# Third mixture: token rows scattered to their expert slots tile by tile during the head

## What is computed

```python
def hierarchical_moe(t, w_group, b_group, w_inner, b_inner, w_gate, w_up, w_down):
    group_p = jax.nn.softmax((t @ w_group + b_group).astype(jnp.float32), axis=-1)
    g_w, g_idx = lax.top_k(group_p, 1)
    inner_all = jnp.einsum('nd,gde->nge', t, w_inner) + b_inner
    inner_logits = jnp.take_along_axis(inner_all, g_idx[:, :, None], axis=1)[:, 0]
    inner_p = jax.nn.softmax(inner_logits.astype(jnp.float32), axis=-1)
    e_w, e_idx = lax.top_k(inner_p, TOP_K_INNER)
    e_w = e_w / jnp.sum(e_w, axis=-1, keepdims=True)
    ...
    for g in range(N_GROUPS):
        hg = jax.nn.silu(jnp.einsum('nd,edf->nef', t, w_gate[g])) * jnp.einsum('nd,edf->nef', t, w_up[g])
        y = y + jnp.einsum('nef,efd->nd', hg * combine[:, g, :, None], w_down[g])
    return y
```

## Time and profile before

| | |
|---|---|
| median of the runs | 2281.05 us (2280.89 to 2281.74) |
| the profiled execution | 2284.3 us |
| its span, first to last instruction | 2282.5 us |
| mean granted clock of TensorE | 0.928 of full speed |
| TensorE matmuls busy | 2049.4 us, 90% |
| VectorE, ScalarE, GpSimd busy | 694.6, 340.2, 70.9 us |
| moved by DMA | 624.69 MB, 274 GB/s over the span |

### The profile page before, as it was taken

One profiled execution on the slowest core, in us unless ns is written; L12 is line 12 of the kernel. 1 busy time (PEld: TensorE's weight loads), 2 busy tenths in 40 slices (PEclk: granted clock), 3 DMA queues, 4 the chain that ended last, 5 costly groups with the idle time before them and its releaser, 6 DMA issues.

```text
span 2282.5 us, 25994 instructions
## 1 busy us (share of the span) xinstructions
PE 2049.4 (90%) x9962; PEld 1113.8 (49%) x9962; DVE 694.6 (30%) x1593; ACT 340.2 (15%) x758; POOL 70.9 (3%) x97
## 2 busy tenths in 40 slices
PE   7999889999999994999999999992899999879772
PEld 3444446555455542846455554451744664634441
DVE  0166646211111114345111111115416333412114
ACT  1133322000000000112000000000122330111110
POOL 0000000000000001000000000001100000100001
PEclk9999879999999997999999999996899559989996
DMA  9911102999999998413999999999222001589995
GB/s 336 360 42 38 56 3 93 399 420 421 421 421 422 421 421 313 148 58 135 412 419 421 421 421 421 421 421 320 69 89 74 1 19 40 224 350 421 420 421 215
DMA packets 144273, 624.69 MB, mean 274 GB/s; under 512 B 13265, under 2 KB 52273, under 8 KB 82769
## 3 DMA queue, kind: packets, MB, share of 16 engines
q1 hardware_dynamic: 119344, 567.24, 62.1%
q0 software_dynamic: 9504, 31.42, 4.1%
q10 hardware_dynamic: 15360, 25.18, 3.0%
HBM read 574.50 MB, written 49.28 MB: 273 GB/s over the span
## 4 chain that ended last, share of the span: by engine, by line
PE 74%; DMA 16%; DVE 6%; ACT 2%; issue 1%; POOL 0%; SPq 0%; POOLq 0%; ACTq 0%; DVEq 0%
PE bank L753 16%; PE bank L780 9%; PE bank L738 9%; DMA ring<-in_moe_w_up_dram 8%; PE bank L639 7%; PE bank L533 7%; DMA ring<-in_w_up_dram 5%; PE bank L504 5%; PE bank L545 4%; PE bank L762 3%; PE bank L892 2%; PE bank L908 1%; DVE h L1148 1%; PE bank L598 1%; PE bank L729 1%
## 5 line engine op out<-in xcount | busy, mean ns | idle before, releaser
L753 PE MATMUL bank<-ring,work 128*64 128x512 f32 x2048 | 454.2, 593 | 5.7 <-DMA ring<-in_moe_w_up_dram 5.3
L1421 DVE TENSOR_TENSOR work<-work,bank 64x512 f32<-64x512 f32 (+1 forms) x96 | 87.0, 906 | 812.3 <-ACT work L1014 812.3
L780 PE MATMUL bank<-ring,work 128*64 128x512 f32 x1280 | 297.1, 602 | 3.6
L753 PEld LDWEIGHTS bank<-ring,work 128*64 128x64 f32 x2048 | 148.4, 137 | 299.5 <-issue 298.9
L738 PEld LDWEIGHTS bank<-work 128*128 128x128 f32 x2112 | 245.7, 191 | 57.2 <-issue 52.7
L738 PE MATMUL bank<-work 128*128 128x128 f32 x2112 | 270.8, 281 | 0.0
L533 PE MATMUL bank<-hT,ring 128*128 128x512 f32 x384 | 169.9, 593 | 0.7 <-ACT work L955 0.7
L780 PEld LDWEIGHTS bank<-ring,work 128*64 128x64 f32 x1280 | 83.5, 137 | 146.1 <-issue 128.7
L1018 ACT ACTIVATE work<-bank 128x512 f32<-128x512 f32 x96 | 57.4, 598 | 623.0 <-PE bank L780 623.0
L762 PE MATMUL bank<-ring,work 128*64 128x256 f32 x1024 | 116.8, 380 | 16.0 <-DMA ring<-in_w_up_dram 15.8
L1014 ACT ACTIVATE work<-bank 64x512 f32<-64x512 f32 (+1 forms) x96 | 49.8, 518 | 507.6 <-PE bank L753 400.3
(11 more groups left out here) (255 smaller groups left out, 1656.0 us busy)
## 6 DMA issues: line engine op xcount, KB each, us to landing
ring<-in_moe_w_gate_dram SPq DMA_DIRECT2D x128, 1024.0 KB, 17.6
ring<-in_moe_w_up_dram SPq DMA_DIRECT2D x128, 1024.0 KB, 19.7
ring<-in_moe_w_down_dram SPq DMA_DIRECT2D x128, 1024.0 KB, 17.6
ring<-in_w_gate_dram SPq DMA_DIRECT2D x32, 1024.0 KB, 20.7
ring<-in_w_up_dram SPq DMA_DIRECT2D x32, 1024.0 KB, 23.1
ring<-in_w_down_dram SPq DMA_DIRECT2D x32, 1024.0 KB, 23.0
y_rows<-work ACTq DMA_DIRECT2D x192, 128.0 KB, 6.9
x_rows<-zeros SPq DMA_DIRECT2D x1, 12800.0 KB, 54.5
```

The lines of the kernel that those rows point to most:

```text
L753: mm = pe.matmul(GU[BLK * a:BLK * a + BLK, :], xT_[:, 4 * kk + k, :], v[:, k, :], start=(kk + k == 0), stop=(kk + k == 4))
L780: mm = pe.matmul(DN[BLK * n:BLK * n + BLK, :], hT_[:, 2 * kk + k, :], v[:, k, 512 * n:512 * n + 512], start=(kk + k == 0), stop=(2 * kk + ...
L1421: dve.tensor_tensor(dealt(hg[:, 0:F], F // P), as_dealt(sg[:, 0:F], F // P), as_dealt(GU[BLK:P, 0:F], F // P), ALU.mult).then_inc(b.hg, 1)
```

## The change

VectorE gets a helper, `rows_of(tt)`, for the third mixture only. It works out the slot rows of one token tile from that tile's one-hots and ranks (expert times 64, plus rank, less one), without the totals over all tiles. Where a rank is beyond the expert's 64 slots, it adds a number so large that the row lies outside `x_rows`, and the scatter leaves such a row out (`bounds_check`, `oob_is_err=False`). It is called for tiles 0 and 1 after `place(1)`, for tile 2 after `place(3)`, and for tile 3 between `copy_rows` and `select(1, 2)`. GpSimd issues the two scatters of a tile when its rows are known, and waits for `routing.indices` only after the reads of `x_rows`. The one-hot `hot2` is formed by `rows_of` and no longer in the long chain. In the branch for overflow blocks, SP gets a wait and an increment more.

```diff
--- before.py
+++ after.py
@@ -114,6 +114,7 @@
         idx = sb("idx", [P, 2 * T], u32)
         top8 = sb("top8", [P, 2 * T, 8], u32)
         ovi = sb("ovi", [P, 32], u32)
+        xidx = sb("xidx", [P, 2 * T], u32)
         bank = [c.enter_context(nc.psum_tensor(f"bank{i}", [P, 512], f32)) for i in range(8)]
         lnp = work[:, 16384:18432]
 
@@ -132,6 +133,7 @@
         out_ready, out_done = sem("out_ready"), sem("out_done")
         rows_zeroed, zero_ready = sem("rows_zeroed"), sem("zero_ready")
         x_zeroed, x_dealt = sem("x_zeroed"), sem("x_dealt")
+        x_rows_known = sem("x_rows_known")
         xg_loaded = [sem(f"xg_loaded{i}") for i in range(2)]
         dve_step = sem("dve_step")
 
@@ -307,6 +309,7 @@
         pos = wk(7572, T * (E + 4)).rearrange("p (t n) -> p t n", t=T)
         rowA = wk(7716, T * E).rearrange("p (t n) -> p t n", t=T)
         oslot = wk(7844, T)
+        xrow, xrank, xover, xjunk = (wk(lo, n) for lo, n in ((7852, 2), (7854, 2), (7856, 2), (7860, 64)))
         sg, hg = wk(3072, 512, (BLK, P)), wk(3584, 512, (BLK, P))
         hgT = wk(4096, 256)
         ysb = [wk(4352 + 512 * i, 512) for i in range(2)]
@@ -456,6 +459,8 @@
                         for q, src in enumerate(expert_units(m, l, e)):
                             u = m.base + q
                             sp.dma_start(ring[u % UNITS][:, :], src).then_inc(m.ov_units, 16)
+                    sp.wait_ge(m.ov.used, m.upb * count + 1)
+                    sp.sem_inc(m.ov.used, 1)
 
             sp.dma_start(con[:, :], t["con"]).then_inc(const_loaded, 16)
             for i in range(T):
@@ -1330,6 +1335,21 @@
                                                 pos[:, tt, n:n + 1].to_broadcast([P, BLK]), ALU.is_equal)
                     ins.then_inc(routing.chosen, 1)
 
+                def rows_of(tt):
+
+                    link(dve.tensor_tensor(hot2[:, tt, :], hots[:, tt, :], hot1[:, tt, :], ALU.subtract))
+                    for k, hot in enumerate((hot1, hot2)):
+                        ins = dve.tensor_tensor_reduce(out=xjunk[:, E * k:E * k + E], in0=hot[:, tt, :],
+                                                       in1=pos[:, tt, 0:E], scale=1.0, scalar=0.0, op0=ALU.mult,
+                                                       op1=ALU.add, accum_out=xrank[:, k:k + 1])
+                    link(ins)
+                    dve.tensor_scalar(xover, xrank, float(MAIN), float(2 * rows_), ALU.is_gt, ALU.mult)
+                    link(dve.scalar_tensor_tensor(out=xrow, in0=top_ids[:, :, tt], scalar=float(BLK), in1=xrank,
+                                                  op0=ALU.mult, op1=ALU.add))
+                    dve.scalar_tensor_tensor(out=xidx[:, 2 * tt:2 * tt + 2], in0=xrow, scalar=-1.0, in1=xover,
+                                             op0=ALU.add, op1=ALU.add).then_inc(x_rows_known, 1)
+                    dve.wait_ge(x_rows_known, tt + 1)
+
                 for tt in range(T):
                     part(tt, 0)
                     if tt == 0:
@@ -1343,12 +1363,17 @@
                         choose(1)
                         place(0)
                         place(1)
+                        if l == 2:
+                            rows_of(0)
+                            rows_of(1)
                     part(tt, 1)
                     normal(tt)
                 choose(2)
                 place(2)
                 choose(3)
                 place(3)
+                if l == 2:
+                    rows_of(2)
                 slots = over_tiles(con[:, C_SLOT:C_SLOT + BLK], BLK)
 
                 def select(buf, e):
@@ -1367,13 +1392,16 @@
 
                 copy_rows(main, 0, 0, 1, P)
                 dve.wait_ge(routing.chosen, T * l + T)
+                if l == 2:
+                    rows_of(3)
                 select(1, 2)
                 dve.tensor_tensor(tokf[:, 0:16].rearrange("p (t n) -> p t n", t=T), gpad[:, :, 0:NG],
                                   over_last(g8[:, :, 0], NG), ALU.subtract)
                 link(dve.tensor_tensor(tokf[:, 16:20], e8[:, :, 1], e8[:, :, 0], ALU.subtract))
                 dve.sem_inc(routing.exp_in, 1)
                 expert_row = over_tiles(expert_ids, E)
-                dve.tensor_tensor(hot2, expert_row, over_last(tokf[:, 56:60], E), ALU.is_equal)
+                if l < 2:
+                    dve.tensor_tensor(hot2, expert_row, over_last(tokf[:, 56:60], E), ALU.is_equal)
                 dve.wait_ge(routing.totals, l + 1)
                 dve.tensor_copy(ovdiff, CT[:, 128:160])
                 link(dve.tensor_scalar(rank, pos[:, :, 0:E], -1.0, None, ALU.add))
@@ -1624,20 +1652,22 @@
                 main = m.main()
                 if l == 0:
                     pool.wait_ge(rows_zeroed, 16)
-                pool.wait_ge(routing.indices, m.l + 1)
                 if l == 2:
                     pool.wait_ge(x_zeroed, 16)
                     for tt in range(T):
+                        pool.wait_ge(x_rows_known, tt + 1)
                         for k in range(2):
                             pool.indirect_dma_start(
                                 out=x_rows, out_offset=bass.IndirectOffsetOnAxis(
-                                    ap=idx[:, T * k + tt:T * k + tt + 1], axis=0),
-                                in_=hn[:, tt, :], in_offset=None).then_inc(x_dealt, 16)
+                                    ap=xidx[:, 2 * tt + k:2 * tt + k + 1], axis=0),
+                                in_=hn[:, tt, :], in_offset=None, bounds_check=rows_ - 1, oob_is_err=False)\
+                                .then_inc(x_dealt, 16)
                     pool.wait_ge(x_dealt, 16 * 2 * T)
                     for q in range(2, E // 2 + 1):
                         if q >= 4:
                             pool.wait_ge(main.xt, main.x0 + 2 * (q - 1))
                         pool.dma_start(xg[q % 2], x_rows[P * q:P * q + P, :]).then_inc(xg_loaded[q % 2], 16)
+                pool.wait_ge(routing.indices, m.l + 1)
                 for s in range(2):
                     pool.wait_ge(main.y_stored[s], main.store0[s] + 32 * E // 2)
                 count = pool.value_load(ovi[0:1, 16:17], min_val=0, max_val=OVF)
```

## The result

The changed kernel takes 2266.14 us (median of seven runs, 2262.97 to 2268.48); the kernel before took 2281.05 us in the median of its seven. The ratio is 0.9937, 95% interval 0.9927 to 0.9947: 12 to 17 us less. The forecast was 2264.9 us in a range of 2261.5 to 2272.0. The profiled execution took 2266.9 us where 2268.1 was worked out.

The account below looks back on a forecast made before the run. The full DMA stream was taken to bound the experts' stretch: 10.0 us of scatter bytes leave, 1.4 us stay, 7.7 us of holes close. That 16.2 us off the 2281.05 us median gives 2264.9 us, range 2261.5 to 2272.

Parts of the forecast that it names:

- The stall and its place: TensorE's single 18.07 us wait for the first expert rows read back would go, with some 7 us to spare.
- What the end is set by: From 1969 us, bytes through the full DMA engines at 0.419 MB/us set the end: 8.75 us per expert against TensorE's 7.38.
- Rival 3: Behind the stall DMA is not the bound; TensorE runs 29 more experts at 7.38 us each, giving 2244 us; chance 0.03.
- The sum: Last up weights in the expert stretch land at 2221.8 us in place of 2238, 16.2 us less.
- the gain by bytes: Scatters leaving the expert stretch take away 10.0 us of DMA time, but 1.4 us (0.6 MB) stays behind 1969 us.
- The holes: DMA time without work early in the expert stretch shrinks from 11.7 to 4.0 us, closing 7.7 us.
- VectorE's new work: 1.2 us per token tile: covered by idle time for tiles 0 to 2, tile 3's delays TensorE's first expert by 1.2 us.
- The scatters on GpSimd: Eight scatters of about 0.95 us each, bounds check taken as 0, issued in three groups near 1944, 1962 and 1965 us.
- rival 4: Bounds-checked scatters are slow on GpSimd, slower overall if above 6.8 us each; at 10 us each, 2307 us; chance 0.04.
- Rival 1: The last scatters land late, up to 22.6 us after issue, stalling TensorE 2 to 7 us: 2267 to 2272 us; chance 0.12.
- Rival 2: GpSimd's scatters and VectorE's head chain hold each other up; VectorE held 7.6 us, giving 2272.5 us; chance 0.06.
- Rival 5: The change does not do what it says: `x_dealt` still comes near 2000 us, 2277 to 2285 us; chance 0.04.

Follow-up runs that it names:

- `late_scatter`: The changed kernel, but GpSimd waits for the end of VectorE's long chain before the first scatter, as the kernel before did; 2281.02 us.
- `chain_late`: The changed kernel, but in the third mixture VectorE runs the long chain over totals behind its part of the first expert; 2263.28 us.
- the second trace: The trace of the changed kernel run again with nothing changed; median 2267.10 us, ratio 0.9942 to the kernel before.

## Why the prediction was right

**The stall and its place.** Right. It stood between the scatters and the first read, `late_scatter` brings it back, and behind it there was no other wait for rows.

**What the end is set by.** Right, and tested from both sides: 4.19 MB put back cost 10.0 us, as priced; 0.52 MB taken off gave 1.7 us for a price of 1.2, too little to be sure of; and 12.2 us of TensorE standing still behind a deep backlog cost at most some 4. Rival 3 is out: the DMA share is 1.02 from 2010 to 2215 us. One sign did not come: TensorE's waits for up weights did not grow from 15.8 us, they were 15.6 us in this trace and 18.0 in the second.

**The sum.** By the chain, the last group came 16.98 us earlier, of which 1.65 us lay ahead of the first expert (1965.07 against 1963.42 us), 1.44 of it ahead of the whole mixture, where nothing was changed. The stretch gives 15.3 us where 16.2 was forecast, and two terms were off in opposite directions. With 103.72 MB the scatters left nothing behind 1969 us, where I had left 0.6 MB, 1.4 us: the gain by bytes is the full 10.0 us. The holes, by 273.00 less 107.92/0.4194 = 15.7 us before and 257.67 less 103.72/0.4194 = 10.4 us after, closed by 5.3 us in place of 7.7. That the sum and the profiled execution came out so near the forecast is in part luck: the gain by bytes was forecast 1.4 us too small and that by holes 2.4 us too large, which nearly cancel, and 1.65 us of the profiled execution's gain came from elsewhere.

**VectorE's new work.** The size was right, its effect not. On VectorE's timeline one tile's rows took 1.03 us (1940.68 to 1941.71 us), where I had 1.2:

```profile
1940.68 0.18 DVE L1340 TENSOR_TENSOR work<-work 128x32 f32<-128x32 f32 x1
1940.90 0.19 DVE L1342 CUSTOM_DVE_ANT_0 work<-work 128x32 f32<-128x32 f32 x1
...
1941.71 0.19 DVE L1340 TENSOR_TENSOR work<-work 128x32 f32<-128x32 f32 x1
...
1943.76 0.69 DVE L1265 SCALAR_TENSOR_TENSOR h<-h,bank 128x512 f32<-128x512 f32 x1 [1.00 <-PE bank L644]
```

Tiles 0, 1 and 2 were covered, with 1.00 and 1.32 us of idle time left. Tile 3 made TensorE wait 2.08 us in place of 1.22, 0.9 us more where 1.2 was forecast. But TensorE's granted clock then fell to its lower level (in the lines below 0.65 and 0.50, the third number from the end), and the eight matmuls of line 743 took 1.98 us in place of 1.16 and the eight of line 785 2.73 in place of 1.94: 1.6 us more:

```profile
1972.00:1974.00 2.00, 1.95 (x10) 1.88 (x11) 0.29 (x1) 0.00 (x0) 0.00 (x0) 0.65 1.00 420
1974.00:1976.00 2.00, 2.00 (x7) 0.69 (x7) 0.69 (x1) 0.00 (x0) 0.00 (x0) 0.50 0.98 406
```

The first expert grew by 2.47 us and not by 1.2. That is the term that was mis-sized; the 1.3 us beyond the forecast are about half of the 2.4 us that the holes did not give, and no row here places the rest. `chain_late`, which left this work in place and moved the long chain behind it out of the way, made the first expert 3.8 us shorter and got 2.6 us or more.

**The scatters on GpSimd.** Right: 0.98 us each in the median where it was 0.95 before, so the bounds check costs next to nothing, and rival 4 is out. Rival 1 did not come: the last scatter had landed 4.1 us after its issue began (1969.13 less 1965.00 us), and 6.5 us in the second trace. Rival 2 came in the direction that the port rule gave it and not in the one that I priced: GpSimd was held for 1.4 us in the fourth scatter, while VectorE's operation, which had begun first (1946.17 against 1946.53 us), kept its 2.00 us, and nobody waited for that scatter. Rival 5 would have shown `x_dealt` near 2000 us.

## What to carry to other kernels

When a stall is removed from a stretch that a stream of weights feeds, price it by the time that the DMA engines stood without work, and add the bytes that leave the stretch. The same stall is worth its whole length where the ring fills up behind it (16.0 us of stall, 15.5 to 17.1 us of loss here) and little while the loads run behind (12.2 us of stall, at most some 4). Small vector work that is put in front of the first product of an expert loop is paid for at the very place where the stream starts; what is needed only at the end belongs behind that product.

## What the hardware showed that I had not expected

- 0.9 us more of waiting went with a fall of TensorE's clock. With a wait of 1.22 us ahead of the first turn it stayed at 2.4 GHz (clock 1.00 from 1970 to 1980 us); with waits of 1.83 to 2.73 us at that place it fell to 1.2 GHz behind them in every trace of the changed kernel and of the variants that keep this order (0.50 from 1974 to 1976 us in the changed one), and cost 1.6 to 1.8 us; without a wait (`chain_late`) it stayed up.
- An indirect DMA on GpSimd took 2.36 us in place of 0.98 while VectorE ran one `scalar_tensor_tensor` of 2.00 us on 128x1024, with both operands in SBUF, and VectorE was not slowed. The Trainium skill, "SBUF — State Buffer", section "Who interferes with whom", counts the two-port modes of copies, casts and `tensor_scalar` and, for two inputs in SBUF, GpSimd's reads as what collides, and infers that descriptor writing does not; here an operation with two SBUF inputs did hold an indirect DMA. That DMA takes its row numbers from `xidx`, which lies in SBUF, so what the section says of GpSimd's reads may cover it; no run here tells the two apart.
- The head alone varied between 81.5 and 84.4 us among executions, with the level of clock that its matmuls got. The three heads below 82 us had a granted clock of 0.87 to 1.00 from 1876 to 1885 us, where the others had 0.50 to 0.64. Among the others, the four near 83 us had their last sixteen matmuls of 128 columns at full clock (2.05 us), the five near 84.2 us at the lower level (3.56 to 3.68 us).
